# Second block: heads in pairs on row and column tiles of TensorE, attention values turned and normalised before the product

## What is computed

```python
h = rms_norm_2(x, attn_norm[l])
p = h @ w_in                                  # 1024 -> cq, ckv, k_rope, mq, mk, mv, rq, rk, rv, rg, three gates
o_mla  = mla_branch(...)                      # 8 heads, q and k 96 wide (64 + 32 rotary), v 64 wide, causal softmax
o_moba = moba_branch(...)                     # 8 heads, q, k and v 64 wide; with 256 tokens: causal softmax
o_ret  = retention_branch(...)                # 4 heads, q and k 64 wide, v 128 wide; decay mask, group norm, silu(rg)
merged = (sigmoid(g_mla) * (o_mla @ w_branch_mla) + sigmoid(g_moba) * (o_moba @ w_branch_moba)
          + sigmoid(g_ret) * (o_ret @ w_branch_ret))
x = x + merged @ w_out
x = x + squared_relu(rms_norm_2(x, mlp_norm[l]) @ w_up) @ w_down
```

## Time and profile before

| what | value |
|---|---|
| median of 3 runs | 1837.16 us (1835.48 to 1840.53) |
| profiled execution | span 1834.2 us; the fastest run is 1.3 us above it, the median 3.0 us |
| TensorE (PE) busy | 1784.0 us, 97% |
| PE weight loads (PEld) | 1458.4 us, 80% |
| VectorE (DVE) busy | 1134.5 us, 62% |
| ScalarE (ACT) busy | 906.8 us, 49% |
| DMA | 264.07 MB, mean 144 GB/s |

### The profile page before, as it was taken

How to read it: one execution, slowest core, us unless ns; L and a number is a source line. 1 busy time by engine, 2 the same in 40 slices (tenths; PEclk the granted TensorE clock), 3 DMA queues, 4 the chain that set the end, 5 groups by cost and what they waited for, 6 DMA issues and landing times. The chain is left out here.

```text
span 1834.2 us, 24040 instructions
## 1 busy us (share of the span) xinstructions
PE 1784.0 (97%) x9216; PEld 1458.4 (80%) x9216; DVE 1134.5 (62%) x2032; ACT 906.8 (49%) x1427; POOL 37.6 (2%) x48
## 2 busy tenths in 40 slices
PE   8999999999998999999999999999999999999998
PEld 4866788777887777777778788799887888779986
DVE  6563566688338446666766675766546666576644
ACT  4332444433336256665655456455434646546533
POOL 0000000000000000000100010000000002000000
PEclk9999999999999999999999999999999999999999
DMA  9555221221335233332444444555555444455562
GB/s 344 193 166 206 93 69 46 69 69 69 138 104 187 89 117 98 121 115 98 157 154 148 140 128 159 182 166 182 194 194 160 133 144 141 167 163 183 184 205 83
DMA packets 114842, 264.07 MB, mean 144 GB/s; under 512 B 5111, under 2 KB 9496, under 8 KB 114536
## 3 DMA queue, kind: packets, MB, share of 16 engines
q1 hardware_dynamic: 111528, 252.52, 41.9%
q0 software_dynamic: 2368, 7.70, 1.3%
q10 hardware_dynamic: 832, 2.30, 0.3%
HBM read 261.46 MB, written 1.05 MB: 143 GB/s over the span
## 5 line engine op out<-in xcount | busy, mean ns | idle before, releaser
L144 DVE TENSOR_TENSOR qw_rest<-weights,qw_lead 128x1024 fp32r<-128x1024 f32 (+2 forms) x428 | 519.8, 1218 | 421.8 <-ACT qw_lead L307 420.1
L307 ACT ACTIVATE qw_lead<-weights 128x1024 fp32r<-128x1024 f32 (+2 forms) x428 | 448.3, 1049 | 508.4 <-PE psum L153 495.7
L153 PE MATMUL psum<-qw_lead,b_h_lead 128*128 128x512 f32 (+1 forms) x480 | 197.3, 411 | 1.7 <-ACT b_mqk L2897 0.9
L153 PE MATMUL psum<-qw_lead,b_h_rest 128*128 128x512 f32 (+1 forms) x480 | 186.7, 389 | 0.0
L153 PE MATMUL psum<-qw_rest,b_h_lead 128*128 128x512 f32 (+1 forms) x480 | 186.1, 388 | 0.0
L153 PE MATMUL psum<-b_h_lead,qw_lead 128*128 128x256 f32 x512 | 145.4, 284 | 2.0 <-DVE b_h_rest L641 2.0
L153 PE MATMUL psum<-b_h_lead,qw_rest 128*128 128x256 f32 x512 | 145.0, 283 | 0.0
L153 PE MATMUL psum<-b_h_rest,qw_lead 128*128 128x256 f32 x512 | 145.0, 283 | 0.0
L153 PE MATMUL psum<-e_h_lead,qw_lead 128*128 128x512 f32 x320 | 141.2, 441 | 1.8 <-DVE e_qT L1420 1.4
L153 PE MATMUL psum<-e_h_lead,qw_rest 128*128 128x512 f32 x320 | 125.9, 393 | 0.0
L153 PE MATMUL psum<-e_h_rest,qw_lead 128*128 128x512 f32 x320 | 125.0, 391 | 0.0
(11 more groups left out here) (489 smaller groups left out, 3438.0 us busy)
## 6 DMA issues: line engine op xcount, KB each, us to landing
weights<-in_w_in SPq DMA_DIRECT2D x48, 1024.0 KB, 5.1
weights<-in_o_w_in SPq DMA_DIRECT2D x32, 1024.0 KB, 5.4
weights<-in_w_mlp_up SPq DMA_DIRECT2D x32, 1024.0 KB, 5.4
weights<-in_w_mlp_down SPq DMA_DIRECT2D x32, 1024.0 KB, 4.9
weights<-in_e_w_in SPq DMA_DIRECT2D x26, 1024.0 KB, 5.2
weights<-in_w_mod SPq DMA_DIRECT2D x24, 1024.0 KB, 6.9
weights<-in_e_w_out SPq DMA_DIRECT2D x8, 1024.0 KB, 4.9
weights<-in_o_w_out SPq DMA_DIRECT2D x8, 1024.0 KB, 4.9
```

What stands on the lines that cost most here:

```text
L144: return eng.tensor_tensor(self.rest[at], src, self.lead[at].bitcast(F32), ALU.subtract)
L153: mm = nc.tensor.matmul(out, l, r, start=start and i == 0, stop=stop and i == 2)
L307: self.core.nc.scalar.activation(self.buf.lead[self.at(u)], self.raw(u), ACT.Copy).then_inc(self.lead_ready, 1)
```

## The change

In `CausalAttention` the heads go in pairs (step 2.8 units for a pair instead of 1.4 for a head). The two heads' score matmuls are issued alternately, into banks 5 and 6. The probabilities are normalised on VectorE before they are turned (`norms`: a reciprocal and two multiplications by a column of 128 and 256 columns). The value product is swapped: the values (64 columns) are stationary, the turned probabilities move (256 and 128 columns), the first head's result goes to PSUM partitions 0 to 63 and the second head's to 64 to 127 of one bank. That result has features on partitions, which is what the branch products read; ScalarE writes its lead (`leads`) and VectorE its rest (`rests`) straight to `oT`, 256 columns for a pair. The heads of a pair share bank 7 for their transposes, and the second head's turn waits for the copy of the first. In `Retention` the score matmuls are paired in the same way; the rest of it stays. The output turn keeps only the two retention blocks, into an array of its own (`low`), which also takes the place of the low-rank `lowT`. Some semaphores are merged or left out (three of the first part among them), and arrays move in memory.

```diff
+    def pairs(self, lag):
+        for j in range(len(self.heads) // 2):
             yield j, self.start + j * self.step + lag
+    def singles(self, lag, apart):
+        for j, at in self.pairs(lag):
+            for i in range(2):
+                yield j, i, 2 * j + i, at + apart * i

     def scores(self, pe):
-            if j >= 2:
-                pe.wait_ge(self.negmax, j - 1)
...
-            nc.tensor.matmul(ps[:, b, 0:P], q(0), k(P), start=True, stop=True)
-            nc.tensor.matmul(ps[:, b, P:3 * P], q(1), k(2 * P), start=True, stop=True).then_inc(self.scored, 1)
+            else:
+                pe.wait_ge(self.negmax, 2 * j)
+            for t, (lo, hi) in enumerate(((0, P), (P, 3 * P))):
+                for i in range(2):
+                    q, k, _ = self.heads[2 * j + i]
+                    mm = nc.tensor.matmul(ps[:, self.banks[i], lo:hi], q(t), k((t + 1) * P), start=True, stop=True)
+                    if t:
+                        mm.then_inc(self.scored, 1)

     def maxima(self, dve):
-        for j, at in self.times(0.45):
+        for j, i, h, at in self.singles(0.45, 0.3):
     def exps(self, act):
-        for j, at in self.times(0.9):
+        for j, i, h, at in self.singles(0.85, 0.3):
+    def norms(self, dve):
+        for j, i, h, at in self.singles(1.3, 0.3):
+            yield at
+            dve.wait_ge(self.exped, 2 * h + 2)
+            self.core.dve_chain(dve, nc.vector.reciprocal(self.rec[:, 2 * h:2 * h + 2], self.tot[:, 2 * h:2 * h + 2]))
+            p = self.prob[:, i, :]
+            for t, (lo, hi) in enumerate(((0, P), (P, 3 * P))):
+                last = nc.vector.tensor_scalar(p[:, lo:hi], p[:, lo:hi], self.rec[:, 2 * h + t:2 * h + t + 1], None, ALU.mult)
+            last.then_inc(self.prob_ready, 1)
     def turns(self, pe):
-        for j, at in self.times(1.6):
+        for j, i, h, at in self.singles(1.8, 0.45):
-            pe.wait_ge(self.exped, 2 * j + 2)
-            if j >= 1:
-                pe.wait_ge(self.probT_ready, j)
+            pe.wait_ge(self.prob_ready, h + 1)
+            if h:
+                pe.wait_ge(self.probT_ready, h)
     def copies(self, act):
-        for j, at in self.times(2.0):
+        for j, i, h, at in self.singles(2.05, 0.45):
     def values(self, pe):
-        for j, at in self.times(2.7):
+        for j, at in self.pairs(2.95):
...
-            nc.tensor.matmul(ps[:, b, 0:w], pt[:, 0:P], v(0), start=True, stop=True)
-            nc.tensor.matmul(ps[:, b, w:2 * w], pt[:, P:2 * P], v(0), start=True, stop=False)
-            nc.tensor.matmul(ps[:, b, w:2 * w], pt[:, 2 * P:3 * P], v(1), start=False, stop=True).then_inc(self.valued, 1)
+            for t in range(LT):
+                for i in range(2):
+                    v, pt = self.heads[2 * j + i][2], self.probT[:, i, :]
+                    mm = nc.tensor.matmul(ps[64 * i:64 * i + 64, self.banks[3], t * P:2 * P], v(t), pt[:, 2 * t * P:(2 + t) * P], start=(t == 0), stop=(t == 1))
+            mm.then_inc(self.valued, 1)
-    def outs(self, dve):
...
+    def leads(self, act):
+        for j, at in self.pairs(3.25):
+            yield at
+            act.wait_ge(self.valued, j + 1)
+            self.core.nc.scalar.activation(self.oT.lead[:, self.block0 + j, :], self.core.ps[:, self.banks[3], 0:SEQ], ACT.Copy).then_inc(self.lead_out, 1)
+    def rests(self, dve):
+        for j, at in self.pairs(3.4):
+            yield at
+            dve.wait_ge(self.lead_out, j + 1)
+            self.oT.take_rest(self.core.nc.vector, np.s_[:, self.block0 + j, :], self.core.ps[:, self.banks[3], 0:SEQ]).then_inc(self.out_done, 1)

 class Retention(Stage):
     def scores(self, pe):
-            b, o = self.banks[j % 2], 64 * (j % 2)
-            q, k = self.rT[o:o + 64, j // 2, :], self.rT[o:o + 64, 2 + j // 2, :]
-            nc.tensor.matmul(ps[:, b, 0:SEQ], k[:, 0:P], q, start=True, stop=True)
-            nc.tensor.matmul(ps[:, b, SEQ:3 * P], k[:, P:SEQ], q[:, P:SEQ], start=True, stop=True).then_inc(self.scored, 1)
+            for t, (lo, hi) in enumerate(((0, SEQ), (SEQ, 3 * P))):
+                for i in range(2):
+                    q, k = self.rT[64 * i:64 * i + 64, n, :], self.rT[64 * i:64 * i + 64, 2 + n, :]
+                    mm = nc.tensor.matmul(ps[:, self.banks[i], lo:hi], k[:, t * P:(t + 1) * P], q[:, t * P:SEQ], start=True, stop=True)
+                    if t:
+                        mm.then_inc(self.scored, 1)

-    o_turn = split_turn(T + "ot_", r.oT, blocks, [branch_at - 5.0 + 0.8 * n for n in range(6)], (3, 4, 5, 6), o_ready, lambda pe: mla.wait_all(pe))
+    o_turn = split_turn(T + "ot_", r.low, blocks, [branch_at - 1.8 + 0.8 * n for n in range(2)], (3, 4), o_ready, lambda pe: mla.wait_all(pe))
```

More of the change, by code:

```diff
@@ L2743, in __init__ @@
         self.rec, self.rec2 = st[:, 6:8], st[:, 20:22]
-        self.low = [st[:, 8 + 4 * i:12 + 4 * i] for i in range(3)]
+        self.low_stat = [st[:, 8 + 4 * i:12 + 4 * i] for i in range(3)]
         self.gst = [st[:, 24 + 8 * i:32 + 8 * i].rearrange("p (t h) -> p t h", t=LT) for i in range(4)]
@@ L2848, in moba_ready @@
         pe.wait_ge(dense.dve_read, 3)
[L2849 to L2853 removed]
+    moba = CausalAttention(core, T + "mo_", [moba_head(h) for h in range(8)], 64 ** -0.5, r.causal, r.prob, r.probT, r.stat[0], r.oT, 4,
+                           (5, 6, 7, 3), t0 + 12.6, 2.8, moba_ready, lambda pe: None)
+    lowT = r.low
     low_meaned, low_rooted, low_scaled = core.sem(T + "low_meaned"), core.sem(T + "low_rooted"), core.sem(T + "low_scaled")
@@ L2858, in low_norm @@
     def low_norm(dve):
-        link, (mean, root, rec) = core.dve_chain, r.low
+        link, (mean, root, rec) = core.dve_chain, r.low_stat
         yield low_at + 0.3
@@ L3032, in second_layer @@
     branch_at = at
-    blocks = [[r.oa[:, t, k * P:(k + 1) * P] for k in (2 * n, 2 * n + 1) for t in range(LT)] for n in range(6)]
+    blocks = [[ret_out[:, t, k * P:(k + 1) * P] for k in (2 * n, 2 * n + 1) for t in range(LT)] for n in range(2)]
     def o_ready(pe, n):
         if n == 0:
-            mla.wait_all(pe)
-        if n == 4:
             pe.wait_ge(gn_done, LT)
@@ L3075, in second_layer @@
         items.append(Item(**span(u, 4, at, 1.0), groups=swapped, src=r.oT, dve=lambda g, b=b: gated(b, g), k0=4 * b,
-                          ready=(lambda pe, q, b=b: o_turn.wait_out(pe, 2 * b + q // 2)) if last else None))
+                          ready=(mla.wait_pair if b == 0 else moba.wait_pair) if last else None))
         u, at = u + 4, at + 4.0
     for j in range(2):
-        items.append(Item(**span(u, 2, at, 1.0), groups=[("tokens", t, 0, BANK) for t in range(LT)], src=r.oT,
-                          dve=lambda g, j=j: gated(2, 2 * j + g), k0=8,
-                          ready=(lambda pe, q: o_turn.wait_out(pe, 4 + q)) if last else None))
+        items.append(Item(**span(u, 2, at, 1.0), groups=[("tokens", t, 0, BANK) for t in range(LT)], src=r.low,
+                          dve=lambda g, j=j: gated(2, 2 * j + g),
+                          ready=o_turn.wait_out if last else None))
         u, at = u + 2, at + 2.0
```

122 lines of the change are left out of this document (54 added, 68 removed).

## The result

The median went from 1836.74 us (1835.48 to 1840.53, four runs) to **1849.01 us** (1844.71 to 1851.87, four runs): a ratio of 1.0059, 95% interval 1.0042 to 1.0075. The change made the kernel slower, by 0.6%, where 1819.7 us had been predicted.

The account below looks back on a forecast made before the run. It took TensorE, busy 97% of the span, as the bound. Scores -9.8, values -7.2, output turn -3.5 and waits +3 made -17.5 us, from 1837.2 to 1819.7 us; range 1812 to 1829.

Parts of the forecast that it names:

- The payload: Cheaper TensorE work in scores, values and output turn, without new waits: -20.5 us.
- Scores in pairs: 12 moba and retention pairs on row tiles: 1.26 us a pair, -9.8 us; best case 1.05 a pair.
- Rival A: Score matmuls on row tiles don't run side by side: 1.65 us a pair, 1824.3 us in all; chance 0.12.
- Values in pairs: 16 pairs of swapped value products on column tiles: 0.89 us a pair, -7.2 us.
- rival B: Weight loads of the value products' column tiles are exposed: 1.22 us a pair, 1825.0 us in all; chance 0.10.
- Output turn: Four of six blocks of output transposes go in each of two layers: -3.5 us.
- The waits added: New TensorE waits at the turns of the attention pairs: +3 us, bounds -1 and +8.
- the square root: In each layer's second moba pair it delays the second head's exponentials; TensorE's wait put at 1.5 us a layer.
- a clock below full: TensorE's granted clock under full, listed as a sign that the forecast is wrong; no size given.
- The merged semaphores: First-part waits whose DMAs are issued long before: 0 us.
- C: Neither row nor column tiles overlap: -3.4 us, 1833.8 us in all, no change that can be told; chance 0.04.
- D: Softmax chain bounds each pair, holding TensorE at both turns behind weight splits: +33.3 us, 1850.0 us in all; chance 0.05.

Follow-up runs that it names:

- e5_scores: The kernel before the change with only the paired score matmuls added; softmax chain, values and output turn stay: 1828.56 us, ratio 0.9950.
- e11_wg: The changed kernel with the gate weights' load in the first part on its own semaphore again: 1845.58 us.
- e12_best_pool: e8 with GpSimd's group-norm work also waiting for the fourth mla normalisation: 1824.09 us, ratio 0.9930.
- e1: The changed kernel with retention's rotation on VectorE due behind the third moba pair's second normalisation: 1837.99 us, ratio 1.0005.
- e9: The changed kernel with GpSimd's group-norm work also waiting for the fourth mla normalisation: 1839.60 us, ratio 1.0011.
- e4: The changed kernel with rotation behind the normalisation, square root behind the pair's exponentials, and normalisation as tensor_tensor: 1841.78 us, ratio 1.0021.
- e8: The changed kernel with rotation, square root and group-norm steps later, turns 0.4 units later, gate weights' own wait again: 1824.24 us, ratio 0.9920.

## Why the prediction was wrong

**The payload was right.** Sum -21.3 against -20.5 us.
- Scores in pairs: 1.05 us a pair, the lower bound, against 1.26. Rival A (1.65) is false: row tiles run side by side, and the eight weight loads cost nothing on top of what four had (their records fill 0.52 us of the pair's 1.05). The Trainium skill ("TensorE: Matmul & The Clock Gate", section "Part 3: Packing small matmuls — row/col tiling") says that a weight load overlaps matmuls in flight when its row group differs; these rows agree.
- Values in pairs: 1.00 against 0.89. Column tiles do run side by side, but not for free: 0.21 us above the 0.79 of full overlap, half of what rival B puts on its exposed loads (1.22). So B's price was double the real one. That the 0.21 us are load time no run shows.
- Output turn: -3.5, as said.
- A slip without effect: the "six records" of an mla head's scores are four; the 768 columns are right.

**The step that failed is "The waits added": +3, measured +18.0** (19.3 at the turns, less the old 1.3), and 20 with the 0.2 us that each wait costs beyond its idle time. The bound was +8. The working named the right chain, with VectorE now between exponentials and turn, and then searched it for two kinds of neighbours only: weight splits, and the square root. It should have listed everything due on VectorE, ScalarE and GpSimd between an exponential and its turn, for every pair. The square root was foreseen (+3 for both layers of which 4.35 came). Not looked for were the rotation (6.5 us in both layers), the group norm's steps on the first mla pair (0.55 us a layer), and GpSimd beside the normalisation (6.9). In the kernel before, weight rests had already been stretched beside GpSimd, with no wait of TensorE behind it. I had not read that stretch. Busy time by stretch (GpSimd is the fifth of the engines) and VectorE in order of time, kernel before:

```profile
1080.00:1090.00 10.00, 10.00 (x57) 8.59 (x56) 8.16 (x20) 7.76 (x16) 7.02 (x4) 1.00 0.47 155
...
1085.91 2.15 DVE L144 TENSOR_TENSOR qw_rest<-weights,qw_lead 128x1024 fp32r<-128x1024 f32 x1 [0.28 <-ACT qw_lead L307]
```

**A term was missing: the clock.** The prediction named "a clock below full" as a sign of being wrong, but gave it no price. It is 6.8 us in the second block of the profiled run, of which about 6.0 come on top of the waits, a third of them. That the waits bring the drops is likely, since before and e5_scores had none in that block; how many come is not fixed by the waits, as e11_wg and e12_best_pool show.

**"The merged semaphores sit in first-part waits ...: 0" was wrong by 1.8 us.** That the loads are issued long before did not mean that they had landed.

**The account.** On the profiled spans, in us: the work -21.3, idle time at the turns +18.0, the 0.2 beyond it for 11 waits more than before +2.2, the clock +6.0, the gate weights' wait +1.8, and the wait on `b_gates` L2788 +1.3 (3.3 against 2.0 before). That is +8.0, of +8.7 measured. The medians lie further apart than the spans (12.3 us), since the profiled run is the fastest of after, with the highest clock (0.993 against 0.9905 in the median, some 4 us).

**The rivals.** C is false, since both kinds of tile overlap. D was on the right side and had the right place, the softmax chain holding TensorE at its turns. Its price came out at the right size (+33.3 predicted, some 26 found with the clock), but for another reason, so that is luck: not each of 16 pairs behind weight splits, but mainly three pairs in each layer behind particular steps, and only 7 of the 32 turns waited over a microsecond. That the chain is too long anywhere (theory 2) is refuted by e1 and e9, where one moved neighbour took its own waits away, and by the moba pairs of e4. e8 brought all waits from 19.3 to 4.5 us, but with later turns as well; the neighbours moved alone, in the form of the change, were not run. D got 0.05. "VectorE is idle 30% of the stretch" was the argument against it, and this is a mean; the waits come from bursts of 3.6 us (the rotation) and 6 us (GpSimd's work) inside it.

## What to carry to other kernels

When a change puts an engine on a path where it was not, list everything that is due on that engine between the two ends of the path, pair by pair, and everything that shares a resource with it: a mean busy share says nothing about that. Price a wait of TensorE above its own length: 0.2 us for each here, and a drop of the clock, up to 1.7 us, behind some of those of 1.8 us and more. Where a tuned order is hand-written, a payload that works (here 21 us) can be turned into a loss by one due time, and moving the neighbours and the turns (25 us between after and e8_best) was worth more than the payload itself.

## What the runs showed of the hardware

- Two row tiles of 64 run side by side: eight fp32 records on alternating tiles cost 1.05 us, as much as four on one.
- Two column tiles of 64 cost 1.00 us for eight records of 768 columns in all per tile, against 0.67 for one head in the old form.
- GpSimd's `tensor_tensor` held up VectorE's operations in SBUF in both forms: 0.55 to 2.68 us for two one-input multiplications, 1.22 to 2.30 for a two-input one. Taking GpSimd away (e9_pool) brought 0.55 back. Where VectorE started first (1088.57), its operation kept its 1.21 us and GpSimd's took 2.35 instead of 1.26. Such a hold-up shows as a longer record, not as idle time.
- A wait of 1.8 us or more was followed by half the clock (starts 0.42 us apart instead of 0.23) in some executions and not in others: the one of 3.27 us at the rotation was not in after and was in e9_pool and e11_wg. With nearly the same waits at the turns, after lost 6.8 us in the second block and e11_wg 15.3.
